# Group norm weights folded into the output projection's weights, and six squared pieces added to two on VectorE before TensorE sums them

## What is computed

```python
def rms_norm(x, g):
    y = x * rsqrt(mean(x * x) + EPS)
    return y * g

mix = concatenate([rms_norm(y_conv, g_grp[:256]),       # short convolution, 256 wide
                   rms_norm(y_attn, g_grp[256:768]),    # windowed attention, 512 wide
                   rms_norm(y_gmlp, g_grp[768:])])      # spatial gating, 256 wide
x = x + einsum('bse,ed->bsd', mix, w_out)               # w_out is 1024 x 1024
x = x + square(relu(rms_norm(x, w_norm2) @ w_ff1)) @ w_ff2
```

## Time and profile before

| what | us |
|---|---|
| median of 3 runs | 2261.01 (2260.59 to 2261.43) |
| the profiled execution, its own time | 2261.24 |
| its span in the trace | 2259.1 |
| TensorE busy | 2223.3 (98%) |
| VectorE busy | 1595.4 (71%) |
| ScalarE busy | 903.4 (40%) |

### The profile page before, as it was taken

The page is one execution under the profiler, slowest core; times in us unless marked ns, Lnnn a source line. Parts: engine busy times, 40 slices in busy tenths (PEclk is TensorE's granted clock), DMA queues, the critical chain, the costliest instruction groups (busy, mean ns, idle before and its releaser), DMA issues.

```text
span 2259.1 us, 34307 instructions
## 1 busy us (share of the span) xinstructions
PE 2223.3 (98%) x13334; PEld 1977.9 (88%) x13334; DVE 1595.4 (71%) x2611; ACT 903.4 (40%) x1714; POOL 128.3 (6%) x223
## 2 busy tenths in 40 slices
PE   7999999999999999999999999999999999999998
PEld 7988888999999988888899878779999999888886
DVE  5327875788777786776852378767877777867767
ACT  5123432456555623233331244234555555223233
POOL 5011000000000000000130100010000000000002
PEclk9999999999999999999999999999999999999999
DMA  5101011345455786536230110124455458846353
GB/s 176 40 26 54 10 52 71 121 160 210 173 201 177 283 304 247 208 127 224 84 74 29 34 46 20 47 96 132 177 182 205 172 204 319 301 172 227 136 215 112
DMA packets 213745, 330.36 MB, mean 146 GB/s; under 512 B 14652, under 2 KB 98144, under 8 KB 213584
## 3 DMA queue, kind: packets, MB, share of 16 engines
q1 hardware_dynamic: 210016, 321.93, 40.2%
q0 software_dynamic: 2704, 3.10, 0.7%
q10 hardware_dynamic: 864, 3.15, 0.4%
HBM read 212.28 MB, written 115.64 MB: 145 GB/s over the span
## 4 chain that ended last, share of the span: by engine, by line
PE 92%; DVE 4%; ACT 1%; issue 1%; DMA 1%; POOL 0%; DVEq 0%; SPq 0%; ACTq 0%; POOLq 0%
PE ps L2041 29%; PE ps L2042 29%; PE ps L2043 29%; PE ps L2226 1%; PE ps L2085 1%; PE ps L2189 1%; PE ps L2209 1%; DVE h_all L1340 1%; PE ps L2128 1%; DMA ff_ops<-row_op 1%; PE ps L2170 1%; DVE xn L1334 0%; DVE w_lo L1319 0%; DVE x L1474 0%; PE ps L2144 0%
## 5 line engine op out<-in xcount | busy, mean ns | idle before, releaser
L2041 PE MATMUL ps<-h_all,w_hi 128*128 128x288 f32 (+1 forms) x1408 | 442.8, 315 | 3.2 <-DVE x L1474 2.7
L2042 PE MATMUL ps<-h_all,w_hi 128*128 128x288 f32 (+1 forms) x1408 | 440.2, 313 | 0.0
L2043 PE MATMUL ps<-h_all,w_lo 128*128 128x288 f32 (+1 forms) x1408 | 440.1, 313 | 0.0
L2041 PE MATMUL ps<-w_hi,h_all 128*128 128x512 f32 (+1 forms) x720 | 275.2, 382 | 1.7 <-ACT vn L1087 0.6
L2043 PE MATMUL ps<-w_hi,h_all 128*128 128x512 f32 (+1 forms) x720 | 269.0, 374 | 0.0
L2041 PEld LDWEIGHTS ps<-h_all,w_hi 128*128 128x128 f32 x1408 | 265.2, 188 | 4.3 <-DVE x L1474 3.1
L2042 PE MATMUL ps<-w_lo,h_all 128*128 128x512 f32 (+1 forms) x720 | 267.8, 372 | 0.0
L2042 PEld LDWEIGHTS ps<-h_all,w_hi 128*128 128x128 f32 x1408 | 265.3, 188 | 0.0
L2043 PEld LDWEIGHTS ps<-h_all,w_lo 128*128 128x128 f32 x1408 | 265.2, 188 | 0.0
L2042 PE MATMUL ps<-w_lo,ring_all 128*128 128x512 f32 x544 | 216.7, 398 | 0.0
L2041 PE MATMUL ps<-w_hi,ring_all 128*128 128x512 f32 x544 | 214.3, 394 | 0.0
(11 more groups left out here) (247 smaller groups left out, 4147.3 us busy)
## 6 DMA issues: line engine op xcount, KB each, us to landing
ff_ops<-row_op SPq DMA_DIRECT2D x128, 512.0 KB, 3.3
w_raw<-in_w_ff SPq DMA_DIRECT2D x128, 256.0 KB, 3.7
ring_all<-ff_ops SPq DMA_DIRECT2D x32, 1024.0 KB, 8.0
ring<-ff_ops SPq DMA_DIRECT2D x32, 1024.0 KB, 8.6
ff_raw<-q SPq DMA_DIRECT2D x96, 256.0 KB, 3.5
b_all<-in_w_ff SPq DMA_DIRECT2D x24, 1024.0 KB, 12.3
w_raw<-in_w_in SPq DMA_DIRECT2D x56, 256.0 KB, 3.9
ring<-ff_raw SPq DMA_DIRECT2D x12, 1024.0 KB, 5.6
```

Source lines behind the costliest of these rows:

```text
L2041: pe.matmul(out, sh, mh, start=first, stop=False)
L2042: pe.matmul(out, sh, ml, start=False, stop=False)
L2043: return pe.matmul(out, sl, mh, start=False, stop=last)
```

## The change

The weight `g` is no longer multiplied into the rows but into the weights of the output projection. A unit's high part becomes the ScalarE copy of `raw * gain` with a gain for each partition (its own channel), and its low part `raw * gain - wh`, one scalar_tensor_tensor on VectorE. `gain_of` gives the column of `gcT` for a unit; `gcT` has two columns more, loaded by two more small transfers of GpSimd, and the broadcast tile `gG` and its load go. `mixed_rows` goes from VectorE: ScalarE now copies the attention rows out of PSUM (`yat`), makes the high parts, and only then the squares. In the gating stage the third VectorE instruction goes. New on VectorE is `square_sums`, which adds pieces 0 and 1 of the squares, and pieces 2 to 5 down to one, in three instructions; TensorE's `group_sums` has two matmuls in place of six, and waits for `sq_sum`, VectorE's signal, in place of ScalarE's `sq_done`.

```diff
-        gcT = place("gcT", [P, 6])
+        gcT = place("gcT", [P, KD])
...
+
+        def gain_of(i):
+
+            if not U_OUT <= i < U_OUT + 16:
+                return None
+            part, j = (i - U_OUT) // 8, (i - U_OUT) % 4
+            k = 2 + j if part else (0, 1, 6, 7)[j]
+            return gcT[:, k:k + 1]
...
+                    load(gcT[:, 6 + c:7 + c], w_group[bass.ds(l, 1), 768 + c * P:768 + (c + 1) * P].rearrange("l p -> p l"),
+                         layer_in)
...
+                    gain = gain_of(i)
+                    if gain is None:
+                        nc.scalar.activation(wh[:, i % 8, 0:cols], raw[:, n % RAW, 0:cols],
+                                             ACT.Copy).then_inc(w_hi_done, 1)
+                    else:
+
+                        act.wait_ge(*layer_in.at("last"))
+                        nc.scalar.activation(wh[:, i % 8, :], raw[:, n % RAW, :], ACT.Copy,
+                                             scale=gain).then_inc(w_hi_done, 1)
...
-                    act.wait_ge(*y_raw.at(t))
-                    nc.scalar.activation(sq6[:, 0:2, :], yg[:].rearrange("p (c n) -> p c n", c=2), ACT.Square,
+                    act.wait_ge(*yg_ready.at(t))
+                    nc.scalar.activation(sq6[:, 0:2, :], u_sb[:, t, :].rearrange("p (c n) -> p c n", c=2), ACT.Square,
                                          accum_out=ssG[:, t:t + 1]).then_inc(*ssg_done.tick(t))
...
                 def gated_back(t):
                     act.wait_ge(*ygT_full.at(t))
+                    act.wait_ge(*ssg_done.at(t))
                     nc.scalar.activation(u_sb[:, t, :], ps[:, 6 + t % 2, 0:256], ACT.Copy).then_inc(*ygT_done.tick(t))
...
-                            act.wait_ge(*ssm_full.at(t - 1))
-                        nc.scalar.activation(sq6[:, 0:2, :], yc[:, :, tile(t)], ACT.Square).then_inc(
-                            *sq_done.tick((t, 0)))
+                            act.wait_ge(*mix_lo.at(t - 1))
+                            act.wait_ge(*sq_done.at(t - 1))
+                        nc.scalar.activation(yat[:], ps[:, 7, :].rearrange("p (h n) -> p h n", h=G4),
+                                             ACT.Copy).then_inc(*yat_done.tick(t))
+                        nc.scalar.activation(hTh[:, 0:2, tile(t)], yc[:, :, tile(t)], ACT.Copy)
                         act.wait_ge(*yat_done.at(t))
-                        nc.scalar.activation(sq6[:, 2:6, :], ps[:, 7, :].rearrange("p (h n) -> p h n", h=G4),
-                                             ACT.Square).then_inc(*sq_done.tick(t))
-
-                        act.wait_ge(*yat_done.at(t))
-                        nc.scalar.activation(hTh[:, 0:2, tile(t)], ycg[:], ACT.Copy).then_inc(*mix_hi.tick((t, 0)))
-                        nc.scalar.activation(hTh[:, 2:6, tile(t)], yat[:], ACT.Copy).then_inc(*mix_hi.tick((t, 1)))
+                        nc.scalar.activation(hTh[:, 2:6, tile(t)], yat[:], ACT.Copy)
                         nc.scalar.activation(hTh[:, 6:8, tile(t)],
                                              u_sb[:, t, :].rearrange("p (c n) -> p c n", c=2),
                                              ACT.Copy).then_inc(*mix_hi.tick(t))
+
+                        if t >= 1:
+                            act.wait_ge(*ssm_full.at(t - 1))
+                        nc.scalar.activation(sq6[:, 0:2, :], yc[:, :, tile(t)], ACT.Square)
+                        nc.scalar.activation(sq6[:, 2:6, :], yat[:], ACT.Square).then_inc(*sq_done.tick(t))
...
+                if gain is None:
+                    V.tensor_tensor(wl[:, slot, 0:cols], raw[:, n % RAW, 0:cols], wh[:, slot, 0:cols].bitcast(F32),
+                                    ALU.subtract).then_inc(w_ready.sem, 1)
+                else:
+
+                    V.scalar_tensor_tensor(wl[:, slot, :], raw[:, n % RAW, :], gain, wh[:, slot, :].bitcast(F32),
+                                           ALU.mult, ALU.subtract).then_inc(w_ready.sem, 1)
...
-            def mixed_rows(t):
-
-                dve.wait_ge(*pv_full.at(t))
-                if t >= 1:
-                    dve.wait_ge(*mix_lo.at(t - 1))
-                V.tensor_tensor(yat[:], ps[:, 7, :].rearrange("p (h n) -> p h n", h=G4),
-                                gcT[:, 2:6].unsqueeze(2).broadcast_to([P, G4, P]), ALU.mult)
-                V.tensor_tensor(ycg[:], yc[:, :, tile(t)], gcT[:, 0:2].unsqueeze(2).broadcast_to([P, 2, P]),
-                                ALU.mult).then_inc(*yat_done.tick(t))
...
+            def square_sums(t):
+
+                dve.wait_ge(*sq_done.at(t))
+                V.tensor_tensor(sq6[:, 0, :], sq6[:, 0, :], sq6[:, 1, :], ALU.add)
+                link(V.tensor_tensor(sq6[:, 2:4, :], sq6[:, 2:4, :], sq6[:, 4:6, :], ALU.add))
+                V.tensor_tensor(sq6[:, 2, :], sq6[:, 2, :], sq6[:, 3, :], ALU.add).then_inc(*sq_sum.tick(t))
...
                     link(V.tensor_tensor(yg[:].rearrange("p (g d) -> p g d", g=4),
                                          ps[:, 2 + t % 2, 0:256].rearrange("p (g d) -> p g d", g=4),
                                          bsp[:, kind, :].unsqueeze(2).broadcast_to([P, 4, HD]), ALU.add))
-                    V.tensor_tensor(yg[:], yg[:], u_sb[:, t, :], ALU.mult).then_inc(*y_raw.tick(t))
-                    dve.wait_ge(*y_raw.at(t))
-                    V.tensor_tensor(u_sb[:, t, :], yg[:], gG[:], ALU.mult).then_inc(*yg_ready.tick(t))
+                    V.tensor_tensor(u_sb[:, t, :], yg[:], u_sb[:, t, :], ALU.mult).then_inc(*yg_ready.tick(t))
...
+                    if i >= 3:
+                        square_sums(i - 3)
...
-                mixed_rows(TS - 2)
                 value_rows(TS - 1)
                 add_sides(0, 2)
...
                 softmax_norm(TS)
                 add_sides(0, 3)
                 mixed_low(TS - 2)
-
-                mixed_rows(TS - 1)
+                square_sums(TS - 2)
+
...
                 group_scale(TS - 2)
+                square_sums(TS - 1)
                 add_sides(0, 5)
-                mixed_rows(TS)
                 group_scale(TS - 1)
                 split(range(U_OUT + 4, U_OUT + 8))
                 add_sides(0, 6)
                 mixed_low(TS)
+                square_sums(TS)
                 add_sides(0, 7)
                 group_scale(TS)
...
-                    pe.wait_ge(*sq_done.at(t - 1))
+                    pe.wait_ge(*yat_done.at(t - 1))
...
-                pe.wait_ge(*sq_done.at(t))
+                pe.wait_ge(*sq_sum.at(t))
                 if t >= 1:
                     pe.wait_ge(*sg_done.at(t - 1))
-                for col, ks in ((0, range(0, 2)), (1, range(2, 6))):
-                    for k in ks:
-                        ins = pe.matmul(ps[:, 1, col:col + 1], sq6[:, k, :], ones[:, 0:1], start=k == ks[0],
-                                        stop=k == ks[-1])
+                pe.matmul(ps[:, 1, 0:1], sq6[:, 0, :], ones[:, 0:1], start=True, stop=True)
+                ins = pe.matmul(ps[:, 1, 1:2], sq6[:, 2, :], ones[:, 0:1], start=True, stop=True)
                 ins.then_inc(*ssm_full.tick(t))
```

More of the change, by code:

```diff
@@ L191, in program @@
         cp_out = place("cp_out", [2, 256], at=base_n + 4096)
-        gG = place("gG", [P, 256], at=base_n + 7168)
         kn = place("kn", [P, 2, P], at=base_n + 8192)
@@ L240, in program @@
         last_op = place("last_op", [P, 2, 2, P], F32R, at=base_l)
-        ycg = place("ycg", [P, 2, P], at=base_l)
         vmix = place("vmix", [P, P], at=base_l + 1024)
         wcT = place("wcT", [P, 2, 3])
-        gcT = place("gcT", [P, 6])
+        gcT = place("gcT", [P, KD])
         bsp = place("bsp", [P, 2, 4])
@@ L334, in program @@
                                                         sig("ve_done"), sig("rln_done"))
-        vn_ready, mixed_full, y_raw, ssg_done = sig("vn_ready"), sig("mixed_full"), sig("y_raw"), sig("ssg_done")
+        vn_ready, mixed_full, ssg_done = sig("vn_ready"), sig("mixed_full"), sig("ssg_done")
         yg_ready, ygT_full, ygT_done = sig("yg_ready"), sig("ygT_full"), sig("ygT_done")
@@ L340, in program @@
         pT_full, pT_done, vmix_set = sig("pT_full"), sig("pT_done"), sig("vmix_set")
-        pv_full, yat_done, sq_done, mix_hi, mix_lo = (sig("pv_full"), sig("yat_done"), sig("sq_done"),
-                                                      sig("mix_hi"), sig("mix_lo", primed=primed))
+        pv_full, yat_done, sq_done, sq_sum = sig("pv_full"), sig("yat_done"), sig("sq_done"), sig("sq_sum")
+        mix_hi, mix_lo = sig("mix_hi"), sig("mix_lo", primed=primed)
         ssm_full, sg_done, rg_done = sig("ssm_full"), sig("sg_done"), sig("rg_done")
@@ L597, in _ @@
                         load(ccin[:], cache_conv[l].rearrange("b j c -> (b j) c"), mid_in)
-                        load(gG[:], w_group[bass.ds(l, 1), 768:1024].broadcast_to([P, 256]), mid_in)
                         load(wnat[:], w_spatial[l].rearrange("g i j -> i g j"), mid_in)
@@ L831, in split @@
```

(17 more changed lines are left out.)

## The result

The changed kernel takes 2274.64 us (2272.89 to 2277.08, 4 runs) against 2261.07 (2260.59 to 2261.43): 13.6 us more, ratio 1.0061 with a 95% interval of 1.0049 to 1.0073. I had forecast 2263.1, in a range of 2256.0 to 2269.0. The profiled execution is the fastest of the four, 2272.89 with a span of 2270.7.

A forecast was written before the change was run, and what follows sets the result against it. TensorE, busy 98% of the span, was taken to bind. Per layer -0.40 (gating stage), -1.40 (result 1) and +2.84 (tail) gave +1.04, two layers +2.1, so 2263.1 us, range 2256.0 to 2269.0.

The forecast's parts named there:

- The passes and the loop: group_sums drops 8 of 12 passes, 0.84 us a call; attention-loop turn falls from 11.26 to 10.42, TensorE still binding.
- The prices: VectorE's added work: square_sums 0.87 us a call, each low part with a gain 0.06 more, 0.25 for four units.
- The gating stage's wait: TensorE's wait at the end of each layer's gating stage falls from 1.16 to 0.7, taken as 0.40 a layer.
- The three waits: TensorE idles each layer some 2.8 us at result 1, 2.2 at group_sums(6) and 4 at group_sums(8).
- the balance: Whole kernel: gains on passes against new waits, +1.04 us a layer, +2.1 for two layers.
- From here I keep the clock of before: The tail, counted from result 1: its times are worked out at the earlier trace's clock.
- Against: the waits near the start followed each other, this one stands alone: Argument against a clock fall behind the tail's 4 us wait: the earlier fall, to 0.72, came where TensorE waited much.
- The sum: Per layer -0.40 at the gating stage, -1.40 at result 1, +2.84 in the tail: +1.04 us, 2263.1 in all.
- a rival, priced at 6.8 us: TensorE's clock falls behind the tail's wait in each layer: 2269.9 us; chance 0.27 shared with the other slow cases.
- the 4 us wait alone: TensorE's wait at group_sums(8) in the tail for VectorE's sums, about 4 us, making result 14 start 2.84 late.
- The likeliest case: Whole kernel: the balance of gains and waits is near zero, 2257 to 2266 us, chance 0.55.
- the slow cases: Dearer sums, a loop bound by VectorE or ScalarE, or a fallen clock: 2266 to 2273 us, chance 0.27.

The follow-up runs named there:

- the filled kernel: The changed kernel plus idle TensorE matmuls ahead of result 0, group_sums(6) and group_sums(8), its waits kept: 2264.34 us against 2261.82 before, ratio 1.0012.
- the kernel with the short wait: The kernel before, with group_sums(8) of each layer also waiting for the addition of result 13: 2269.65 us against 2261.32, ratio 1.0037.
- the early copy: The changed kernel with VectorE's sums for tiles 0 to 3 only and copy_qT(TS) ahead of tile 7's exponentials: 2257.26 us against 2263.45 before, ratio 0.9971.
- the four-tile kernel: The changed kernel with VectorE's sums for tiles 0 to 3 only, six matmuls for the others: 2259.13 us against 2263.45 before, ratio 0.9978.

## Why the prediction was wrong

**The passes and the loop: right.** A call of four passes, two products of one column, takes 0.37 us in the loop (237.37 to 237.74) where I had 0.42, and the loop's turn became 10.36 us (10.42 forecast; 11.26 in the earlier trace rows):

```profile
235.60 1.23 DVE L1440 TENSOR_REDUCE mx<-ps 128x8 f32<-128x1024 f32 x1 [0.19 <-PE ps L2186]
...
245.96 1.23 DVE L1440 TENSOR_REDUCE mx<-ps 128x8 f32<-128x1024 f32 x1 [0.34 <-PE ps L2186]
```

VectorE has 0.34 and 0.19 us to spare a turn (0.25 forecast).

**The prices: right.** From the first to the third addition of `square_sums` it is 0.65 us (243.88 to 244.53), and VectorE's next instruction starts at 244.74, so that the whole takes 0.86 (0.87 forecast). A low part with a gain takes 0.744 against 0.684, the 0.06 that I took:

```profile
243.88 0.28 DVE L1482 TENSOR_TENSOR sq<-sq 128x128 f32<-128x128 f32 x1
244.08 0.42 DVE L1483 TENSOR_TENSOR sq<-sq 128x256 f32<-128x256 f32 x1
244.53 0.29 DVE L1484 TENSOR_TENSOR sq<-sq 128x128 f32<-128x128 f32 x1
```

The rule from the Trainium skill's page "VectorE: DVE Perf Modes", section "The DRAIN you can't avoid", by which the three would have cost more, is not borne out by these rows: the second addition starts 0.20 us after the first, which lasts 0.28; the section itself adds that an op that is not held starts earlier. The gating stage's wait fell to 0.7 from 1.16, as said.

**The three waits: right in place and nearly in size.** 2.40 at result 1 (2.8 forecast), 1.91 at `group_sums(6)` (2.2), 3.89 at `group_sums(8)` (4), and the same in layer 1: 8.2 a layer for a forecast of 9.0. With the waits filled the balance came out at +2.5 us, where I had +2.1.

**The failed step: "From here I keep the clock of before", held up by "Against: the waits near the start followed each other, this one stands alone".** The sum put the price of a fallen clock at nothing. I had it as a rival, priced at 6.8 us from the earlier trace rows, and argued it away; it also was tied to the 4 us wait alone. In its place the runs showed that a lone wait of 1.45 us suffices (8.3 us for two, with 2.9 of wait), and that all three waits of a layer can do it. The work lost to the clock was 11.1 us in the profiled execution, and 10 to 11 by the medians of the filled kernel. The likeliest case was built from waits at full clock, even the rival stopped at one fall a layer (2269.9), and both the range, up to 2269.0, and the slow cases, up to 2273, ended below the 2274.64 measured.

**What stays open.** The same wait does not always bring the same fall. In the kernel with the short wait five executions lie between 2266.92 us at a mean clock of 0.998 and 2273.03 at 0.993. The wait at `group_sums(6)` was 1.91 us in both layers of the profiled execution; behind it the clock was 0.59 in layer 0, and in layer 1:

```profile
1424.00:1428.00 4.00, 2.09 (x16) 1.74 (x16) 2.83 (x7) 1.91 (x5) 0.00 (x0) 1.00 0.00 0
1428.00:1432.00 4.00, 4.00 (x19) 3.22 (x18) 2.28 (x4) 1.60 (x4) 0.00 (x0) 1.00 0.00 0
```

What decides between the two was not tried. It fits that the four runs of the changed kernel spread over 4.2 us and the four of before over 0.8. Why the early copy gave 6.2 us and not 8 is open too; the interval reaches to 9.

## What to carry to other kernels

When TensorE is busy 98% of the time, an edit that trades its passes for work on another engine must be judged by each wait that it opens, not by the sum of passes and waits alone: a wait costs its length and can have a stretch at half clock behind it. Here a wait of 1.45 us cost 4.2, while those of 0.65 and 1.1 us had none behind them in the profiled executions. Do such work only in the turns in which the other engine is ahead: the same three additions for tiles 0 to 3 gain 0.2 to 0.3%, for all nine they lose 0.6%. And follow a late chain to the next consumer before removing one wait of it: the wait at result 1 came back at `values(6)`.

## What the runs showed of the hardware

TensorE's granted clock fell from 2.4 to 1.2 GHz behind single waits of 1.45 to 3.9 us in work that was unbroken before, and the stretches of 4 us behind them stand at 0.50 to 0.72. Waits of 0.4 to 1.2 us, those of the gating stage in the earlier trace rows and of result 1 in the four-tile kernel among them, left it at 1.00. The Trainium skill, page "TensorE: Matmul & The Clock Gate", section "Why this matters for your kernels", warns of gaps between bursts of matmuls; the traces agree, with shorter gaps than I had taken for harmful. Matmuls whose results nobody reads hold the clock up at no cost of their own as long as they end before the wait does: 2274.6 us became 2264.3.
